# The weight sums of a seven-product output projection, made by transfers that add to their target

## The chip, the cores and the metric

The kernel runs on one core of a Trainium2 chip. A core has a matrix engine (TensorE, PE in the profile, with a weight-load side PEld), a vector engine (VectorE, DVE), a scalar engine (ScalarE, ACT), a general engine (GpSimd, POOL) and SyncE (SP), which here only issues transfers. They run their own instruction lists and meet at semaphores. The metric is the device time of one execution in microseconds; a comparison goes by the median of several executions.

## The reference

One layer: an input projection, two token mixers side by side, a gated merge, one output projection and a layer norm over residual plus projection. Everything is float32. The part that the change touches is the second and third line from the end:

```
ua = jnp.einsum('blc,cd->bld', (oa.astype(x.dtype) * jax.nn.silu(za)), w_up_a)
ub = jnp.einsum('blc,cd->bld', ob * jax.nn.silu(zb), w_up_b)
merged = jax.nn.sigmoid(ga) * ua + jax.nn.sigmoid(gb) * ub
y = jnp.einsum('bld,de->ble', merged, w_out)
return layer_norm(ALPHA * x + y, ln_g, ln_b)
```

There are 512 tokens and 1024 channels, so `merged` is 512 x 1024 and `w_out` 1024 x 1024.

## The kernel before

A float32 product is made of three matmuls of rounded parts. Each operand is split into a high part (rounded to the matmul's format, by ACT) and a low part (the operand less its high part, by DVE or GpSimd); the three matmuls are high x high, high x low and low x high. So every weight, and every sum of weights, costs a transfer, a rounding on ACT and a subtraction on GpSimd or DVE before TensorE can use it.

The work is cut into units of 256 output columns (`UNITS`); unit `u` is quartered, and a quarter number `q` = 4u to 4u + 3 is the clock by which each engine's program is written: at each `q` every engine does what its `side(q)` and the tables (`OUT_HI_AT`, `OUT_HI_THEN`, `OUT_LO_AT`) say. The last units, `up0` to `up3` (q = 108 to 123), are the two up-projections. Their results are merged on DVE (`merge(m)`, m = 0 to 7, 128 channels each) into `mix`, rounded on ACT (`round_merged`), and given a low part on DVE (L1739). `sum_rows(j)` makes four sums of quarters of `mix` into `s_raw`, `round_sums(j)` rounds them (L1208), and `sum_rows_lo(j)` makes their low part (L1762).

The output projection is a 2 x 2 block product done with seven block products instead of eight (the Strassen-Winograd scheme): token halves and even or odd channels on one side, four blocks `b11`, `b12`, `b21`, `b22` of `w_out` on the other. The products run in the order `b11`, `b21`, `t1`, `t2`, `b22`, `t3`, `t4` (`OUT_WEIGHTS`). Each is 24 matmuls: two token tiles (`i`) of four pieces (`j`) of three matmuls, L965 to L968. The four `t` are sums of weight blocks:

- t1 = b12 - b11, t2 = b22 - t1, t3 = b22 - b12, t4 = b21 - t2, each one made by DVE in `sum_out` (L1783) from blocks of 128 x 2048 floats, 1 MB.

`out_raw(name)` says where a raw block or sum lies: `z_a`, `z_b`, or one of the two halves of `w_raw`, the ring through which the weight units come. SP loads the blocks with `load_out` (L586): `b11` and `b12` before `up0`, `b12` again into `z_a` once b11's low parts are done, `b21` once the low parts of `up2` are done and `b22` after those of `up3`. ACT rounds block n in two halves, `split_out_hi(n, half)` (L1224). GpSimd makes the low part in four pieces, `split_out_lo(n, piece)` (L2072). Both have an order of their own, `HI_ORDER` and `LO_ORDER`, in which b22 comes before t2. ACT is in order: in its program behind the last quarter stand `round_merged(7)`, `keep_first` (L1229, a copy of product b11 to `first_sum`, which product b21 waits for before it adds to the same bank), `round_sums(3)`, the roundings of t2, t3 and t4, and then `move_u` (L1234), which copies the partial sum `u` to the bank in which product t3 goes on; t3 waits for it (`u_moved`).

In the tail each token block t gets its row statistics on DVE (L1793, L1796), 1 / sigma on ACT, and is scaled by halves: on DVE (`normalise_half`, L1840 and L1843), or, for the halves in `ON_POOL`, by one operation on ACT and two on GpSimd.

Of the kernel before, what the change touches and what calls it, by code (L numbers as in the profile page):

```python
# [115 lines left out]
def hybrid_kernel(nc, x_t, x_tok, w_units, w_kiwi, b_cols, b_ia, b_vb, lb_cols, g_cols, rel_bias,  # L116
                  ln_g, ln_b, one_hot, ident, causal, tree_masks, out):
    with ExitStack() as ctx:
# [179 lines left out]
        out_in = {n: sem(f"out_in_{n}") for n in OUT_BLOCKS}  # L298
        out_sum, out_hi, out_lo, out_lo_dve = (sem(n) for n in ("out_sum", "out_hi", "out_lo", "out_lo_dve"))
# [175 lines left out]
        def out_raw(name):  # L475

            u2, u3 = UNITS.index("up2"), UNITS.index("up3")
            ring = {"b21": u2, "t4": u2, "b22": u3}
            if name in ring:
                return w_raw[:, ring[name] % 2, :].rearrange("p (j n) -> p j n", j=PAIRS)  # L480
            return z_a[:] if name in ("b11", "t3") else z_b[:]

        def wait_out_raw(eng, name):

            if name in OUT_BLOCKS:
                eng.wait_ge(out_in[name], 16)
            else:
                eng.wait_ge(out_sum, ("t1", "t2", "t3", "t4").index(name) + 1)

        LO_ORDER = (0, 1, 2, 4, 3, 5, 6)  # L490
# [11 lines left out]
        HI_ORDER = (0, 1, 2, 4, 3, 5, 6)  # L502
# [60 lines left out]
        def _(sp):  # L563
# [21 lines left out]
            def load_out(name, dst):  # L585
                sp.dma_start(dst, w_units[NMAIN - 1 + OUT_BLOCKS.index(name)]  # L586
                             .rearrange("p (j n) -> p j n", j=PAIRS)).then_inc(out_in[name], 16)

            for u in range(2, NMAIN):
                if UNITS[u] == "up0":  # L590
                    sp.wait_ge(o_lo_done, 4)
                    load_out("b11", z_a[:])
                    load_out("b12", z_b[:])
# [380 lines left out]
        def _(act):  # L974
# [342 lines left out]
            for q in range(4 * NMAIN):  # L1317
# [10 lines left out]
                for v in range(3, NMAIN):  # L1328
                    if q - hi_quarter(v) in (0, 1):
                        split_hi(v, q - hi_quarter(v))  # L1330
# [26 lines left out]
                if m is not None:  # L1357
                    round_merged(m)
                    if m % 2:
                        round_sums(m // 2)  # L1360
# [22 lines left out]
        def _(dve):  # L1383
# [358 lines left out]
            def sum_rows(j):  # L1742

                if j:
# [4 lines left out]
                nc.vector.tensor_tensor(s_raw[:, 0, :], even[:, HALF:], odd[:, HALF:], ALU.add).then_inc(s_raw_done, 1)  # L1749
# [7 lines left out]
                                        ALU.subtract).then_inc(s_raw_done, 1)  # L1757
# [6 lines left out]

            def sum_out(name):

                dst = out_raw(name)
                if name == "t1":
                    wait_out_raw(dve, "b11")
                    wait_out_raw(dve, "b12")  # L1770
                    a, b = z_b[:], z_a[:]
                elif name == "t2":
                    wait_out_raw(dve, "b22")
                    wait_out_lo(dve, 2, 4)
                    a, b = out_raw("b22"), z_b[:]
                elif name == "t3":
                    dve.wait_ge(out_in["b12"], 32)
                    a, b = out_raw("b22"), z_a[:]
                else:
                    wait_out_lo(dve, 1, 4)  # L1780
                    dve.wait_ge(out_sum, 2)
                    a, b = out_raw("b21"), out_raw("t2")
                nc.vector.tensor_tensor(dst, a, b, ALU.subtract).then_inc(out_sum, 1)  # L1783
# [34 lines left out]
            def rows_12(i):  # L1818
# [6 lines left out]
                nc.vector.tensor_tensor(c12_bank[i][:], c12_bank[i][:], u_sum[:, i, :], ALU.add).then_inc(pre_12, 1)  # L1825

            def rows_22(i):

                t = 2 + i
                wait_y_full(dve, "t3", i)  # L1830
                link(nc.vector.tensor_tensor(m6_bank[i][:], c21_bank[i][:], y_sb[:, t, 512:], ALU.add))
                with_residual(c21_bank[i][:], t, 0, c21_bank[i][:]).then_inc(pre_21, 1)
                row_stats(t, 1)
# [18 lines left out]
            def side(q):  # L1852
# [70 lines left out]
                if q == T1_AT:  # L1923
                    sum_out("t1")
# [61 lines left out]
        def _(pool):  # L1986
# [79 lines left out]

            def split_out_lo(n, piece):
# [4 lines left out]
                nc.gpsimd.tensor_tensor(lo, out_raw(name)[:, piece, :], hi.bitcast(F32), ALU.subtract).then_inc(out_lo, 1)  # L2072

# [8 lines left out]
            for q in range(4 * NMAIN):  # L2082
                side(q)
                for n, piece in OUT_LO_AT.get(q, ()):
                    split_out_lo(n, piece)
            for n in LO_ORDER[3:]:
                for piece in range(4):
                    split_out_lo(n, piece)
            pool.wait_ge(ln_in, 32)
# [73 lines left out]
```

## Time and profile before

| | us |
|---|---|
| median of three executions | 460.0 (459.72 to 460.41) |
| the profiled execution | 459.87 |
| its span, first to last instruction | 457.8 |
| what lies around the span | 2.1 |

The profile is one execution. The page gives each engine's busy time; the views in order of time give each instruction's start and duration in us from the start of the span, and, in square brackets, how long its engine stood idle before it and what ended that. The duration of an instruction on DVE or GpSimd includes what it stands for access to its data. Matmuls overlap: one is shown with 0.39 us but the next begins 0.23 us later. For a transfer the view shows the issue; the time to landing stands in the table of issues.

### The profile page before, as it was taken

How to read it: one execution, taken by the hardware profiler on the slowest of the kernel's cores; microseconds unless marked ns; L12 is line 12 of the kernel's file. 1: busy time of each engine (PE TensorE's matmuls, PEld its weight loads, DVE VectorE, ACT ScalarE, POOL GpSimd, SP SyncE). 2: the span in 40 equal slices, each digit the busy share in tenths (PEclk: the TensorE clock that was granted, in tenths of full speed). 3: DMA queues.
4: the chain of work that ended last, by engine and by line, in shares of the span. 5: the costliest groups of instructions: out<-in, count | busy, mean ns of one | idle time of the engine just before them, and what ended most of it. 6: DMA issues, size and time to landing. Idle time of an engine off the chain costs nothing.

```text
span 457.8 us, 7703 instructions
## 1 busy us (share of the span) xinstructions
PE 445.2 (97%) x2946; PEld 362.8 (79%) x2946; DVE 319.7 (70%) x585; ACT 236.7 (52%) x398; POOL 186.3 (41%) x175
## 2 busy tenths in 40 slices
PE   9999999999999999999999999999999999999793
PEld 7778888888888788888888887887888888877582
DVE  4546589999999853346989994870642058899977
ACT  5735455253345746285777475735775343624421
POOL 0444432582259813581004000000066494655962
PEclk9999999999999999999999999999999999999997
DMA  8808122256023620205020222041066254231013
GB/s 255 297 23 295 69 79 93 92 155 214 0 93 98 179 94 1 93 1 169 16 94 1 95 93 93 1 129 59 1 226 227 99 181 186 93 130 55 0 46 137
DMA packets 16867, 48.77 MB, mean 107 GB/s; under 512 B 2456, under 2 KB 4288, under 8 KB 16192
## 3 DMA queue, kind: packets, MB, share of 16 engines
q1 hardware_dynamic: 16592, 48.10, 31.5%
q8 instruction: 23, 0.38, 0.3%
q10 hardware_dynamic: 240, 0.20, 0.2%
q14 instruction: 12, 0.10, 0.1%
HBM read 44.09 MB, written 2.11 MB: 101 GB/s over the span
## 4 chain that ended last, share of the span: by engine, by line
PE 85%; DVE 9%; POOL 2%; issue 2%; ACT 2%; DVEq 0%; POOLq 0%
PE bank L635 21%; PE bank L636 21%; PE bank L637 21%; PE bank L798 2%; PE bank L783 2%; POOL w_lo L2072 2%; PE bank L881 2%; PE bank L834 2%; DVE s_lo L1762 1%; PE bank L774 1%; PE bank L773 1%; PE bank L965 1%; PE bank L968 1%; PE bank L967 1%; PE bank L925 1%
## 5 line engine op out<-in xcount | busy, mean ns | idle before, releaser
L1998 POOL TENSOR_TENSOR w_lo<-w_raw,w_hi 128x512 fp32r<-128x512 f32 x84 | 112.3, 1363 | 157.2 <-ACT w_hi L976 157.1
L635 PE MATMUL bank<-x_hi,w_hi 128*128 128x512 f32 x336 | 133.0, 396 | 0.0
L636 PE MATMUL bank<-x_lo,w_hi 128*128 128x512 f32 x336 | 131.2, 390 | 0.0
L637 PE MATMUL bank<-x_hi,w_lo 128*128 128x512 f32 x336 | 130.9, 390 | 0.0
L635 PEld LDWEIGHTS bank<-x_hi,w_hi 128*128 128x128 f32 x336 | 63.1, 188 | 13.9 <-issue 0.8
L637 PEld LDWEIGHTS bank<-x_hi,w_lo 128*128 128x128 f32 x336 | 63.1, 188 | 13.6
L636 PEld LDWEIGHTS bank<-x_lo,w_hi 128*128 128x128 f32 x336 | 63.1, 188 | 12.2
L976 ACT ACTIVATE w_hi<-w_raw 128x1024 fp32r<-128x1024 f32 (+2 forms) x63 | 62.5, 1012 | 8.0 <-PE bank L637 5.7
L1063 ACT ACTIVATE prob<-prob,nmax 128x128 f32<-128x128 f32 (+3 forms) x32 | 17.7, 555 | 41.6 <-DVE nmax L1517 41.5
L1493 DVE MAX8 best<-score 128x8 f32<-128x256 f32 (+2 forms) x48 | 26.8, 559 | 1.1
L1505 DVE COPY prob_t<-bank 128x128 f32<-128x128 f32 (+3 forms) x32 | 14.3, 486 | 19.0 <-PE bank L783 18.9
L1494 DVE MATCH_REPLACE8 score<-best,score 128x256 f32<-128x256 f32 (+2 forms) x48 | 26.1, 543 | 0.0
L635 PE MATMUL bank<-w_hi,x_hi 128*128 128x512 f32 x64 | 25.3, 395 | 0.0
L637 PE MATMUL bank<-w_hi,x_lo 128*128 128x512 f32 x64 | 25.0, 390 | 0.0
L636 PE MATMUL bank<-w_lo,x_hi 128*128 128x512 f32 x64 | 24.9, 390 | 0.0
L635 PE MATMUL bank<-o_hi,w_hi 128*128 128x512 f32 x64 | 24.9, 389 | 0.0
L636 PE MATMUL bank<-o_lo,w_hi 128*128 128x512 f32 x64 | 24.9, 389 | 0.0
L637 PE MATMUL bank<-o_hi,w_lo 128*128 128x512 f32 x64 | 24.9, 389 | 0.0
L1053 ACT ACTIVATE relus<-bank 128x256 f32<-128x256 f32 (+2 forms) x24 | 10.5, 489 | 21.2 <-PE bank L763 21.2
L2016 POOL TENSOR_TENSOR logit<-t,pen 128x256 f32<-128x256 f32 x24 | 17.4, 737 | 9.1 <-DVE nmax L1517 9.1
L1483 DVE SCALAR_TENSOR_TENSOR score<-relus,w_idx,score 128x256 f32<-128x256 f32 (+2 forms) x21 | 15.6, 743 | 7.8 <-ACT relus L1053 6.1
L1697 DVE TENSOR_TENSOR w_lo<-w_raw,w_hi 128x512 fp32r<-128x512 f32 x32 | 20.6, 684 | 0.0
(267 smaller groups left out, 824.2 us busy)
## 6 DMA issues: line engine op xcount, KB each, us to landing
w_raw<-in_w_units SPq DMA_DIRECT2D x58, 512.0 KB, 4.7
z_a<-in_w_units SPq DMA_DIRECT2D x2, 1024.0 KB, 5.2
w_raw<-in_w_units SPq DMA_DIRECT2D x2, 1024.0 KB, 4.8
y_sb<-in_x_tok SPq DMA_DIRECT2D x4, 512.0 KB, 4.7
out<-y_sb SPq DMA_DIRECT2D x8, 256.0 KB, 2.0
x_raw_hi<-in_x_t SPq DMA_DIRECT2D x4, 256.0 KB, 5.2
x_raw_lo<-in_x_t SPq DMA_DIRECT2D x4, 256.0 KB, 6.3
t_turned<-t_row SPq DMA_DIRECT2D x1, 1024.0 KB, 9.7
```

The costliest lines, as they stand in the source:

```text
L635: nc.tensor.matmul(dst, a_hi, b_hi, start=first, stop=False)
L636: nc.tensor.matmul(dst, a_hi, b_lo, start=False, stop=False)
L637: return nc.tensor.matmul(dst, a_lo, b_hi, start=False, stop=last)
L976: nc.scalar.activation(split_target(u, kiwi_hi, x_hi, w_hi)[:, k, :], raw(u)[:, k, :], ACT.Copy).then_inc(done, 1)
L1063: nc.scalar.activation(prob[:, i % 4, 0:n], prob[:, i % 4, 0:n], ACT.Exp, bias=nmax[:, i % 4:i % 4 + 1], scale=-1.0, accum_out=prob_sum[:, ...
L1483: ins = nc.vector.scalar_tensor_tensor(out=score[b][:], in0=relus[:, i % 2, 0:n], scalar=w, in1=score[b][:], op0=ALU.mult, op1=ALU.add)
L1493: link(nc.vector.max(best8[:], score[b][:]))
L1494: link(nc.vector.match_replace(score[b][:], best8[:], score[b][:], TAKEN))
L1505: nc.vector.tensor_copy(prob_t[:, i % 4, 0:n], turn_bank[i % 2][:, 0:n]).then_inc(turn_out[i % 2], 1)
L1697: nc.vector.tensor_tensor(split_target(u, kiwi_lo, x_lo, w_lo)[:, k, :], raw(u)[:, k, :], split_target(u, kiwi_hi, x_hi, w_hi)[:, k, :].bi ...
L1998: nc.gpsimd.tensor_tensor(split_target(u, kiwi_lo, x_lo, w_lo)[:, k, :], raw(u)[:, k, :], split_target(u, kiwi_hi, x_hi, w_hi)[:, k, :].bi ...
L2016: nc.gpsimd.tensor_tensor(logit[:, i % 2, n - band:n], t5[:, h, 2 * P - band:], pen[b][:, n - band:] if b else causal_sb[:], ALU.add).then ...
```

## The change

The signs of the scheme are turned so that all sums of weights are additions: t1 = b12 + b11, t2 = b22 + b11 + b12, t3 = b12 + b22, t4 = b11 + b12 + b22 + b21. On the other side some sums of `mix` and three sums of results turn from add to subtract or back, on the same shapes. `sum_out` and its four calls on DVE are gone. In their place GpSimd issues transfers that add a block from memory to what already lies in the target (`add_block`, `accum_op=ALU.add`): one for t1, two for t2, three for t4, one for t3. Each waits for the load of its target and for the add before it to the same target. SP loads the first term: `b22` as t2 into `z_a`, `b11` as t4 into the ring half in which b21 lay, `b12` as t3 into `z_b`, the last two ahead of the loads of `y_sb`. The orders `HI_ORDER` and `LO_ORDER` become plain 0 to 6, so t2 is split ahead of b22. Both halves of the rounding of `up3` go to q = 116, the rounding of b21 goes from q = 118 to q = 116 and ahead of `round_sums`, its low parts from 119 to 118. Of token block 1 both halves are now scaled by GpSimd.

```
-OUT_HI_THEN = {118: ((1, 0), (1, 1))}
-OUT_LO_AT = {110: ((0, 0), (0, 1), (0, 2), (0, 3)), 119: ((1, 0), (1, 1), (1, 2), (1, 3)), 121: ((2, 2), (2, 3))}
-T1_AT, T1_LO_AT = 106, 121
-ON_POOL = ((), (1,), (1,), ())
+OUT_HI_THEN = {116: ((1, 0), (1, 1))}
+OUT_LO_AT = {110: ((0, 0), (0, 1), (0, 2), (0, 3)), 118: ((1, 0), (1, 1), (1, 2), (1, 3)), 121: ((2, 2), (2, 3))}
+ADD_AT = {101: (("t1", "b11"),), 114: (("t2", "b11"),), 117: (("t2", "b12"),), 121: (("t4", "b12"),)}
+T1_LO_AT = 121
+ON_POOL = ((), (0, 1), (1,), ())
...
+        TERMS = {"t1": 2, "t2": 3, "t3": 2, "t4": 4}
...
             wait_out_lo(sp, 0, 4)
-            sp.wait_ge(out_sum, 1)
-            load_out("b12", z_a[:])
+            load_out("t2", "b22")
             wait_lo(sp, UNITS.index("up2"), 4)
-            load_out("b21", out_raw("b21"))
+            load_out("b21", "b21")
             wait_lo(sp, UNITS.index("up3"), 4)
-            load_out("b22", out_raw("b22"))
+            load_out("b22", "b22")
+            wait_out_lo(sp, 1, 4)
+            load_out("t4", "b11")
+            wait_out_lo(sp, 2, 4)
+            load_out("t3", "b12")
...
-            split_out_hi(4, 0)
-            split_out_hi(4, 1)
+            split_out_hi(3, 0)
+            split_out_hi(3, 1)
             round_merged(KT - 1)
             keep_first(0)
             keep_first(1)
             round_sums(PAIRS - 1)
-            for n in (3, 5, 6):
+            for n in (4, 5, 6):
                 for half in range(2):
                     split_out_hi(n, half)
...
             sum_rows(PAIRS - 1)
-            sum_out("t2")
             sum_rows_lo(PAIRS - 1)
-            sum_out("t3")
             dve.wait_ge(ln_in, 32)
             rows_11(0)
-            sum_out("t4")
             rows_11(1)
...
+            def add_block(name, block):
+
+                pool.wait_ge(out_in[name], 16)
+                if added[name]:
+                    pool.wait_ge(out_add[name], 16 * added[name])
+                added[name] += 1
+                nc.gpsimd.dma_start(out_raw(name), out_block(block), accum_op=ALU.add).then_inc(out_add[name], 16)
...
             for n in LO_ORDER[3:]:
                 for piece in range(4):
                     split_out_lo(n, piece)
+                if n == 3:
+                    add_block("t4", "b22")
+                    add_block("t3", "b22")
+                elif n == 4:
+                    add_block("t4", "b21")
```

The first place is ACT's list from the rounding of `up3` (`w_hi<-w_raw`) to that of `mix` 5. A name in brackets is what the instruction waits for. Before:

```order
L976 ACTIVATE w_hi<-w_raw 128x1024 [waits part_done,w_in0_0]
L1203 ACTIVATE odd_hi<-mix 128x512 [waits mix_done]
L1208 ACTIVATE s_hi_hi<-s_raw 128x1024 [waits s_raw_done]
L976 ACTIVATE w_hi<-w_raw 128x1024 [waits w_in0_1]
L1203 ACTIVATE even_hi<-mix 128x256 [waits mix_done]
L1224 ACTIVATE x_hi<-w_raw 128x1024 [waits part_done,out_in_b21]
L1224 ACTIVATE x_hi<-w_raw 128x1024
L1224 ACTIVATE w_hi<-z_b 128x1024 [waits part_done,out_sum]
L1224 ACTIVATE w_hi<-z_b 128x1024
L1203 ACTIVATE odd_hi<-mix 128x512 [waits mix_done]
```

And after the change:

```order
L983 ACTIVATE w_hi<-w_raw 128x1024 [waits part_done,w_in0_0]
L983 ACTIVATE w_hi<-w_raw 128x1024 [waits w_in0_1]
L1210 ACTIVATE odd_hi<-mix 128x512 [waits mix_done]
L1231 ACTIVATE x_hi<-w_raw 128x1024 [waits part_done,out_in_b21]
L1231 ACTIVATE x_hi<-w_raw 128x1024
L1215 ACTIVATE s_hi_hi<-s_raw 128x1024 [waits s_raw_done]
L1210 ACTIVATE even_hi<-mix 128x256 [waits mix_done]
L1231 ACTIVATE w_hi<-z_b 128x1024 [waits part_done,out_add_t1,out_in_t1]
L1231 ACTIVATE w_hi<-z_b 128x1024
L1210 ACTIVATE odd_hi<-mix 128x512 [waits mix_done]
```

The second half of `up3` and both halves of b21 (`x_hi<-w_raw`) stand now ahead of the rounding of the s sums (`s_hi_hi<-s_raw`), with b21's load (`out_in_b21`) as a wait in front of it.

The second place is GpSimd's list from the low parts of b21 (`x_lo<-w_raw`) to those of t4, the last ones. Before:

```order
L2072 TENSOR_TENSOR x_lo<-w_raw,x_hi 128x512 [waits out_hi] x4
L2072 TENSOR_TENSOR w_lo<-z_b,w_hi 128x512 [waits out_hi] x2
L2072 TENSOR_TENSOR w_late<-w_raw,w_late 128x512 [waits out_hi] x4
L2072 TENSOR_TENSOR w_lo<-z_b,w_hi 128x512 [waits out_hi] x4
L2072 TENSOR_TENSOR x_lo<-z_a,x_hi 128x512 [waits out_hi] x4
L2072 TENSOR_TENSOR x_lo<-w_raw,x_hi 128x512 [waits out_hi] x4
```

And after the change, from the last low part of `up3` on:

```order
L1984 TENSOR_TENSOR w_lo<-w_raw,w_hi 128x512 [waits hi_done]
L2060 TENSOR_TENSOR x_lo<-w_raw,x_hi 128x512 [waits out_hi] x4
L2060 TENSOR_TENSOR w_lo<-z_b,w_hi 128x512 [waits out_hi] x2
L2068 DMA w_raw<-in_w_units 128x2048 [waits out_in_t4]
L2060 TENSOR_TENSOR w_lo<-z_a,w_hi 128x512 [waits out_hi] x4
L2068 DMA w_raw<-in_w_units 128x2048 [waits out_add_t4,out_in_t4]
L2068 DMA z_b<-in_w_units 128x2048 [waits out_in_t3]
L2060 TENSOR_TENSOR w_late<-w_raw,w_late 128x512 [waits out_hi] x4
L2068 DMA w_raw<-in_w_units 128x2048 [waits out_add_t4,out_in_t4]
L2060 TENSOR_TENSOR x_lo<-z_b,x_hi 128x512 [waits out_hi] x4
L2060 TENSOR_TENSOR x_lo<-w_raw,x_hi 128x512 [waits out_hi] x4
```

Four of the seven adding transfers (`DMA ... <-in_w_units`) stand between the low parts, each behind the waits in its brackets, and the low parts of t2 (`w_lo<-z_a`) have moved ahead of those of b22 (`w_late`).

## Rows read from the trace of the kernel before

**Rows 1.** Busy time by engine, from the page (busy us, share, instructions).

```profile
PE 445.2 (97%) x2946; PEld 362.8 (79%) x2946; DVE 319.7 (70%) x585; ACT 236.7 (52%) x398; POOL 186.3 (41%) x175
```

**Rows 2.** TensorE in order of time (start us, us, line, operation; idle before).

```profile
406.77 0.39 PE L965 MATMUL bank<-x_hi,even_hi 128*128 128x512 f32 x1
...
408.58 0.39 PE L968 MATMUL bank<-x_hi,even_lo 128*128 128x512 f32 x1
409.96 0.50 PE L965 MATMUL bank<-x_hi,even_hi 128*128 128x512 f32 x1 [0.98 <-DVE even_lo L1739]
...
413.30 0.39 PE L968 MATMUL bank<-x_hi,even_lo 128*128 128x512 f32 x1
414.23 0.50 PE L965 MATMUL bank<-x_hi,odd_hi 128*128 128x512 f32 x1 [0.54 <-ACT first_sum L1229]
...
426.39 0.40 PE L968 MATMUL bank<-w_hi,s_lo 128*128 128x512 f32 x1
429.07 0.50 PE L965 MATMUL bank<-w_hi,s_hi_lo 128*128 128x512 f32 x1 [2.28 <-POOL w_lo L2072]
...
429.64 0.39 PE L968 MATMUL bank<-w_hi,s_lo 128*128 128x512 f32 x1
430.32 0.50 PE L965 MATMUL bank<-w_hi,s_hi_lo 128*128 128x512 f32 x1 [0.29 <-POOL w_lo L2072]
...
449.98 0.39 PE L968 MATMUL bank<-x_hi,odd_lo 128*128 128x512 f32 x1
```

**Rows 3.** VectorE (DVE) in order of time, 401 to 425 us.

```profile
401.04 1.50 DVE L1749 TENSOR_TENSOR s_raw<-mix 128x256 f32<-128x256 f32 x1
...
406.92 0.69 DVE L1732 TENSOR_TENSOR bank<-bank,gate_a_lo 128x512 f32<-128x512 f32 x1
...
417.71 2.28 DVE L1783 TENSOR_TENSOR z_b<-w_raw,z_b 128x2048 f32<-128x2048 f32 x1
...
421.04 2.29 DVE L1783 TENSOR_TENSOR z_a<-w_raw,z_a 128x2048 f32<-128x2048 f32 x1
...
424.70 3.18 DVE L1783 TENSOR_TENSOR w_raw<-w_raw,z_b 128x2048 f32<-128x2048 f32 x1
```

**Rows 4.** ScalarE (ACT) in order of time, 391 to 433 us.

```profile
391.00 1.06 ACT L1208 ACTIVATE s_hi_hi<-s_raw 128x1024 fp32r<-128x1024 f32 x1 [2.33 <-DVE s_raw L1756]
...
427.92 2.01 ACT L1224 ACTIVATE x_hi<-w_raw 128x1024 fp32r<-128x1024 f32 x2 [2.55 <-DVE w_raw L1783]
432.62 0.60 ACT L1234 ACTIVATE bank<-u_sum 128x512 f32<-128x512 f32 x1 [2.70 <-DVE u_sum L1822]
```

**Rows 5.** GpSimd (POOL) in order of time, 421 to 435 us.

```profile
421.17 9.10 POOL L2072 TENSOR_TENSOR w_lo<-z_b,w_hi 128x512 fp32r<-128x512 f32 x4 [4.79 <-ACT w_hi L1224]
430.22 5.03 POOL L2072 TENSOR_TENSOR x_lo<-z_a,x_hi 128x512 fp32r<-128x512 f32 x4
```

**Rows 6.** SP, the queue that issues transfers, in order of time.

```profile
384.95 11.23 SPq L586 DMA_DIRECT2D w_raw<-in_w_units  x2
406.96 1.75 SPq L623 DMA_DIRECT2D y_sb<-in_x_tok  x4
```

**Rows 7.** Issues (KB each, us to landing) and two windows (DMA share, GB/s last).

```profile
z_a<-in_w_units SPq DMA_DIRECT2D x2, 1024.0 KB, 5.2
...
z_b<-in_w_units SPq DMA_DIRECT2D x1, 1024.0 KB, 6.8
...
338.00:348.00 10.00, 10.00 (x46) 8.29 (x45) 2.70 (x2) 6.01 (x7) 7.06 (x5) 1.00 0.84 315
384.00:396.00 12.00, 12.00 (x55) 9.94 (x54) 10.57 (x14) 6.00 (x7) 6.37 (x6) 1.00 0.25 89
```

**Rows 8.** VectorE in order of time, the last 11 us of the span.

```profile
447.11 0.76 DVE L1840 SCALAR_TENSOR_TENSOR bank<-bank,aggr,ln_gb 128x512 f32<-128x512 f32 x1
447.90 0.75 DVE L1843 SCALAR_TENSOR_TENSOR y_sb<-bank,rstd,ln_gb 128x512 f32<-128x512 f32 x1
...
451.00 0.69 DVE L1793 BATCH_NORM_STATS2 stats<-bank 128x6 f32<-128x512 f32 x1
```

More of the change, by code:

```diff
@@ L480, in out_raw, with out_block @@
                 return w_raw[:, ring[name] % 2, :].rearrange("p (j n) -> p j n", j=PAIRS)
-            return z_a[:] if name in ("b11", "t3") else z_b[:]
+            return z_a[:] if name in ("b11", "t2") else z_b[:]
+        def out_block(name):
+            return w_units[NMAIN - 1 + OUT_BLOCKS.index(name)].rearrange("p (j n) -> p j n", j=PAIRS)
+        TERMS = {"t1": 2, "t2": 3, "t3": 2, "t4": 4}
         def wait_out_raw(eng, name):
[L485 to L490, printed above, removed]
+            eng.wait_ge(out_in[name], 16)
+            if name in TERMS:
+                eng.wait_ge(out_add[name], 16 * (TERMS[name] - 1))
+        LO_ORDER = (0, 1, 2, 3, 4, 5, 6)
         def wait_out_lo(eng, n, pieces):
@@ L591, in _ @@
                     sp.wait_ge(o_lo_done, 4)
-                    load_out("b11", z_a[:])
-                    load_out("b12", z_b[:])
+                    load_out("b11", "b11")
+                    load_out("t1", "b12")
                 if u >= 3:
@@ L1328, in _ @@
                 for v in range(3, NMAIN):
-                    if q - hi_quarter(v) in (0, 1):
+                    if v == NMAIN - 1 and q == hi_quarter(v):
+                        split_hi(v, 0)
+                        split_hi(v, 1)
+                    elif v < NMAIN - 1 and q - hi_quarter(v) in (0, 1):
                         split_hi(v, q - hi_quarter(v))
@@ L1358, in _ @@
                     round_merged(m)
-                    if m % 2:
-                        round_sums(m // 2)
                 for n, half in OUT_HI_THEN.get(q, ()):
                     split_out_hi(n, half)
-            split_out_hi(4, 0)
-            split_out_hi(4, 1)
+                if m is not None and m % 2:
+                    round_sums(m // 2)
+            split_out_hi(3, 0)
+            split_out_hi(3, 1)
             round_merged(KT - 1)
@@ L1748, in sum_rows @@
                 n = 4 * j
-                nc.vector.tensor_tensor(s_raw[:, 0, :], even[:, HALF:], odd[:, HALF:], ALU.add).then_inc(s_raw_done, 1)
+                nc.vector.tensor_tensor(s_raw[:, 0, :], even[:, HALF:], odd[:, HALF:],
+                                        ALU.subtract).then_inc(s_raw_done, 1)
                 nc.vector.tensor_tensor(s_raw[:, 2, :], even[:, 0:HALF], even[:, HALF:],
@@ L1756, in sum_rows @@
                 nc.vector.tensor_tensor(s_raw[:, 3, :], odd[:, 0:HALF], s_raw[:, 1, :],
-                                        ALU.subtract).then_inc(s_raw_done, 1)
+                                        ALU.add).then_inc(s_raw_done, 1)
             def sum_rows_lo(j):
@@ L1763, in sum_rows_lo @@
                                         ALU.subtract).then_inc(s_lo_done, 1)
[L1765 to L1783, printed above, removed]
             def first_sum_lo():
@@ L1824, in rows_12 @@
                 dve.wait_ge(early_12, i + 1)
-                nc.vector.tensor_tensor(c12_bank[i][:], c12_bank[i][:], u_sum[:, i, :], ALU.add).then_inc(pre_12, 1)
+                nc.vector.tensor_tensor(c12_bank[i][:], c12_bank[i][:], u_sum[:, i, :], ALU.subtract).then_inc(pre_12, 1)
             def rows_22(i):
@@ L1830, in rows_22 @@
                 wait_y_full(dve, "t3", i)
-                link(nc.vector.tensor_tensor(m6_bank[i][:], c21_bank[i][:], y_sb[:, t, 512:], ALU.add))
+                link(nc.vector.tensor_tensor(m6_bank[i][:], y_sb[:, t, 512:], c21_bank[i][:], ALU.subtract))
                 with_residual(c21_bank[i][:], t, 0, c21_bank[i][:]).then_inc(pre_21, 1)
@@ L2065, in side @@
                         far_factors(p)
+            added = {name: 0 for name in TERMS}
             def split_out_lo(n, piece):
@@ L2085, in _ @@
                     split_out_lo(n, piece)
+                for name, block in ADD_AT.get(q, ()):
+                    add_block(name, block)
             for n in LO_ORDER[3:]:
```

14 lines of the change are left out of this document (6 added, 8 removed).

## The prediction, made before the changed kernel had run

> **What bounds the kernel now.** I read the page's busy times first. TensorE is busy 445.2 us of a span of 457.8 us [rows 1], so a change that leaves the matmuls alone can win only where TensorE stands idle, or after its last matmul. Next I listed TensorE's instructions of the last 60 us in order of time [rows 2]. The output projection begins at 406.77. Nine matmuls later (408.58) the pace is (408.58 - 406.77) / 8 = 0.226 us each, so one of the seven products, 24 matmuls, takes 5.44 us when nothing stops it. Against that pace there are four gaps: 408.58 + 0.23 to 409.96 is 1.15 us (the low half of `mix` 6, from DVE), 413.30 + 0.23 to 414.23 is 0.70 us (`first_sum`), 426.39 + 0.23 to 429.07 is 2.45 us, and 429.64 + 0.23 to 430.32 is 0.45 us. The last two are product t2 waiting for the low parts of its weight sum. Together they are 4.75 us. The last matmul ends at 449.98 + 0.39 = 450.37, and the 7.4 us to the end of the span belong to the layer norm and the last store.
>
> Why t2 is late is in the other engines' rows. DVE makes the sum t2 from 417.71, t3 from 421.04, t4 from 424.70, 2.3 to 3.2 us each [rows 3]. ACT rounds t2 after its sum, and GpSimd's four low parts take 9.10 us from 421.17, where the next four take 5.03 us, 1.26 us each [rows 5]: the big DVE sums and GpSimd's operations get in each other's way.
>
> **What the change removes.** First, the three late sums on DVE, 2.28 + 2.29 + 3.18 = 7.75 us [rows 3], and an earlier one, t1. With them goes the late t2: its raw sum comes from transfers issued around 385 and 394, ACT rounds it right behind the last projection (after 406.8), and GpSimd makes its low parts before those of b22. From 409 four pieces, even at the slowed 9.10 us, end by 418, while TensorE reaches t2 at 406.77 + 3 x 5.44 = 423.1 or later. Both t2 gaps go: **-2.90 us**. What is late next is discussed under t3. Sign changes (subtract for add, on equal tiles) cost nothing: the same DVE operation on the same shape.
>
> Second, both halves of token block 1's last scaling now go to GpSimd. DVE no longer does 0.76 + 0.75 us there at 447.11 and 447.90 [rows 8]. The statistics of the last block start at 451.00, though TensorE ended at 450.37; with 1.5 us less ahead of them they start 0.6 us sooner: **-0.6 us**. ACT's second scaling and GpSimd's two further operations fit before 451.
>
> **What it adds.** Seven adding transfers of 1 MB from GpSimd's queue, and two more plain 1 MB loads. No row shows a transfer from GpSimd or an adding one. The nearest row is a plain load of the same bytes: 5.2 us from issue to landing alone, 6.8 us with another just ahead [rows 7]. The window 338 to 348 moved 315 GB/s at a DMA share of 0.84, that is 375 GB/s at full share; 1.05 MB then need 2.8 us of moving, and 5.2 - 2.8 = 2.4 us are fixed. An adding transfer has a source to read like the load, and its target to read besides. So its moving time is between 2.8 us (the target's read hidden) and 5.6 us (the two reads one after the other), and an adder slower than the stream would go above it. I take 4.0 us, between the ends, because one of the two reads stays on the chip and never meets the weight loads at their source; both ends are kept. The issue on GpSimd I take at 1 us, between an SP issue (0.33 us) and a GpSimd tile operation (1.26 us).
>
> Now the places. *The first add* (t1) is issued near 348 and needed at 396: hidden at any of these sizes. *The second and third* (t2 += b11, t2 += b12): the first goes out at about 385, together with SP's load of b21 (384.95 [rows 6]). Sharing the engines, that load lands near 385 + 2.4 + 2 x 2.8 = 393 instead of 390. This matters because ACT's rounding of b21 has been moved ahead of the rounding of the s sums, which ran at 391.00 [rows 4]. ACT now stands at b21 from 389 to 393, rounds 2 us, and the s sums come at 395 instead of 391. Queued behind are DVE's low part of the s sums and the merges of `mix` 4 and 5; both move back by some 2.7 us, and then the four small s sums (1.50 us where GpSimd is busy, as at 401.04 [rows 3]) follow. The merge of `mix` 6, at 406.92 in the trace, comes 0.8 to 1.5 us later, and TensorE's gap for it grows from 1.15 to some 2.0 us: **+0.9 us**. The 0.70 us gap stays.
>
> *t4 and t3* are the tight ones. In the new order the load of t4 goes out when b21's low parts are done (403) and lands at 408; t4 += b12 is issued at about 409 beside the load of t3 and the four loads of `y_sb` (406.96 in the trace [rows 6]), so it moves at half speed and lands at 409 + 8.0 + 2.4, near 419. Then t4 += b22 and t3 += b22 go out, and move one after the other: t4 near 426.5, t3 near 430.5. t4 += b21 is issued when b22's low parts are done, near 427, and lands behind t3 at 434.7. ACT rounds t4 (2.01 us, as at 427.92) and only then moves `u` into the bank (0.60 us, as at 432.62 [rows 4]), and product t3 waits for that move. So t3 can start at 434.7 + 2.0 + 0.6 + 0.1 = 437.4. TensorE comes to it at 406.77 + 5 x 5.44 + 2.0 + 0.7 = 436.7 with the gaps above and two or three tenths of slow restarts. The chain ends within half a microsecond of the need: at 4.0 us of moving time it costs **0 to +0.5 us**, at 2.8 us nothing. I put it at 0.
>
> **Sum**, on the profiled execution (459.87 us, span 457.8): -2.90 - 0.6 + 0.9 + 0 = -2.6, so 457.3 us. The profiled execution lies 0.13 us under the median of 460.0, so the forecast is **457.4 us**.
>
> **Rivals.** (A) *The adding transfers are nearly as cheap as loads* (2.8 to 3.3 us). Then b21 and the t4 chain both have room, the +0.9 shrinks to about 0, and even the 1.15 us gap goes, since the sums left DVE and ACT is on time; 460.0 - 2.9 - 0.6 - 1.15 = 455.4 us. For it: engines were far from full (DMA share 0.25 from 384 to 396 [rows 7]). Against: two reads. (B), *on the other side: the t4 chain takes the place of t2*. The decisive point is a moving time of about 4.4 us. Above it, each further microsecond counts four to five times, since four adds stand in a row before the rounding of t4 (one of them at half speed) and the move of `u` stands behind it. At 5.6 us the last add lands near 443 and t3 starts near 445.7, while TensorE, its `mix` 6 gap grown by 1.5 us, comes to it at 437.3: 8.4 us of standing, and 460.0 - 2.9 - 0.6 + 1.5 + 8.4 = **466 us**; at 4.8 us the same count gives about 461.5. For it: nothing hides the second read if the engines are full, and y loads, t3 load and adds together ask for 3 x 2.8 + 4 x 5.6 = 31 us of moving in the 28 us from 409 to 437. Against: the share of the target's read that overlaps the source's. The Trainium skill, "Collectives: The Full Stack", in "The bandwidth ceiling: the fold count and why AG ≠ RS ≠ AR", says a reducing transfer reads two sources on one ring and runs at half a copy's rate; by that rule the time would be that of rival B, and no row here shows it. (C) *The third place:* the adds go out later than issued, because GpSimd's own descriptor work meets DVE; it would look like B, and is in its chance. (D) The change does not relieve t2 or the wins and losses cancel: 459.1 to 460.9.
>
> **How the numbers follow.** The forecast (moving time 3.5 to 4.3 us, 456 to 459 us) gets 0.33, rival A 0.17, D 0.10, B 0.40: some 0.24 of it up to 467, the rest above. The likeliest single case is faster, though its lead is small, so the range must hold both signs: from 455.0 (just under A's time) to 467.0 (B with the two reads one after the other), which leaves out an adder slower than that. The forecast's own range is 456 to 459. Bounds of 0.2% (0.9 us) are about what a measurement of this kernel tells from no change: faster 0.50, same 0.10, slower 0.40.
>
> **What would show it.** Right: no gap of TensorE before t2's matmuls; t2's low parts on GpSimd done by 418; the adding transfers landing 7 to 8 us after issue; the end of the last matmul 2 us sooner and the tail 0.6 us shorter. Wrong: a gap before the first matmul of t3 with ACT's `u` move as releaser and t4's last add landing after 436 (B); a gap over 2.5 us in b11 (the b21 rounding costs more than said); GpSimd standing more than 1 us per issue.

## The result, and the profile of the changed kernel

The changed kernel takes 467.61 us (median of four executions, 465.59 to 468.75) where the kernel before took 460.21 us beside it. The ratio is 1.015, with a 95% interval of 1.0127 to 1.0172. The forecast was 457.4 us with a range up to 467.0: wrong in its sign and just outside its range. The profiled execution took 468.75 us with a span of 466.9 us, 9.1 us more than the 457.8 before. It is the slowest of the four (the medians differ by 7.4 us): its mean granted clock is 0.981, that of the others 0.986 to 0.991, so the books below are those of this one execution. Two executions of the experiments further down (746.7 and 904.07 us) fell in a second, much slower state and are left out of all medians and ratios.

TensorE in order of time, to be read beside [rows 2] (start us, us, line, operation; idle before and what ended it):

```profile
406.79 0.39 PE L972 MATMUL bank<-x_hi,even_hi 128*128 128x512 f32 x1
...
408.60 0.39 PE L975 MATMUL bank<-x_hi,even_lo 128*128 128x512 f32 x1
413.14 0.80 PE L972 MATMUL bank<-x_hi,even_hi 128*128 128x512 f32 x1 [4.15 <-DVE even_lo L1749]
413.73 0.63 PE L974 MATMUL bank<-x_lo,even_hi 128*128 128x512 f32 x1
...
418.58 0.39 PE L974 MATMUL bank<-x_lo,even_hi 128*128 128x512 f32 x1
...
440.57 0.39 PE L975 MATMUL bank<-w_late,s_lo 128*128 128x512 f32 x1
446.43 0.80 PE L972 MATMUL bank<-x_hi,s_hi_hi 128*128 128x512 f32 x1 [5.48 <-ACT bank L1241]
...
452.48 0.39 PE L975 MATMUL bank<-x_hi,s_lo 128*128 128x512 f32 x1
...
459.99 0.39 PE L975 MATMUL bank<-x_hi,odd_lo 128*128 128x512 f32 x1
```

The output projection starts where it did (406.79, before 406.77). The two gaps before t2 and the one of `first_sum` are gone, 2.90 and 0.70 us. Two others are in their place: 4.31 us before the tenth matmul of the output projection (1.15 before) and 5.63 us before product t3 (none before). Behind each, most matmuls follow each other at 0.43 us instead of 0.227: the 13 from 413.14 to 418.58 take 5.44 us where 2.95 is the pace, the 14 from 446.43 to 452.48 take 6.05 us where 3.18 is. The clock column names it (windows; the granted clock is the first of the last three columns, then DMA share and GB/s):

```profile
412.00:418.00 6.00, 4.86 (x11) 3.81 (x12) 4.72 (x7) 3.43 (x5) 4.84 (x5) 0.50 0.98 317
...
440.00:450.00 10.00, 4.52 (x13) 3.27 (x12) 2.50 (x5) 3.44 (x6) 8.03 (x7) 0.78 0.24 61
```

A granted 0.50 is the level of 1.2 GHz, and TensorE had stood for 4.3 us ahead of it. (The second window holds the gap and the end of the half clock, hence its 0.78.) The books, then: -2.90 - 0.70 + 3.16 (the gap of `mix` 6) + 2.49 (half clock behind it) + 5.63 (the gap of t3) + 2.87 (half clock) - 0.9 (the tail: 466.9 - 460.38 = 6.5 us, before 7.4) = +9.65 against a measured +9.1. The half microsecond left over is in the kernel before: from its first to its last matmul start of the output projection are 449.98 - 406.77 = 43.21 us, and 167 steps of 0.227 us with the gaps of 4.75 us make only 42.66. Most of the rest is in the slower first steps behind its four gaps (0.34 us each instead of 0.227, as behind 409.96).

### The profile page after: what moved, and what is told of

The parts are those of the page before. It is cut to its first block, busy times and chain, and to the rows that moved or that the text cites. A ratio compares the mean times of both kernels' runs of the same rounds, so it can differ in the third digit from the quotient of the medians.

```text
span 466.9 us, 7708 instructions
## 1 busy us (share of the span) xinstructions
PE 449.7 (96%) x2946; PEld 366.8 (79%) x2946; DVE 311.6 (67%) x579; ACT 237.6 (51%) x399; POOL 187.4 (40%) x184
## 4 chain that ended last, share of the span: by engine, by line
PE 83%; DMA 10%; POOL 2%; DVE 2%; issue 2%; ACT 1%; POOLq 0%; DVEq 0%
PE bank L642 21%; PE bank L643 20%; PE bank L644 20%; DMA w_raw<-in_w_units 7%; DMA z_a<-in_w_units 3%; PE bank L790 2%; PE bank L805 2%; PE bank L888 2%; PE bank L841 2%; PE bank L781 1%; PE bank L780 1%; PE bank L972 1%; POOL x_lo L2060 1%; PE bank L974 1%; PE bank L932 1%
## 5 line engine op out<-in xcount | busy, mean ns | idle before, releaser
L1984 POOL TENSOR_TENSOR w_lo<-w_raw,w_hi 128x512 fp32r<-128x512 f32 x84 | 111.1, 1349 | 153.3 <-ACT w_hi L983 153.2
L1742 DVE TENSOR_TENSOR bank<-bank,gate_a_hi 128x512 f32<-128x512 f32 x4 | 2.8, 694 | 32.2 <-PE bank L644 32.2
## 6 DMA issues: line engine op xcount, KB each, us to landing
w_raw<-in_w_units POOLq DMA_DIRECT2D x3, 1024.0 KB, 11.3
y_sb<-in_x_tok SPq DMA_DIRECT2D x4, 512.0 KB, 12.4
```

Source lines behind the costliest of these rows:

```text
L1984: nc.gpsimd.tensor_tensor(split_target(u, kiwi_lo, x_lo, w_lo)[:, k, :], raw(u)[:, k, :], split_target(u, kiwi_hi, x_hi, w_hi)[:, k, :].bi ...
```

## The two gaps, read in the other engines' rows

**The gap of 4.31 us.** DVE and GpSimd in order of time, to be read beside [rows 3] and [rows 5]:

```profile
396.11 0.70 DVE L1742 TENSOR_TENSOR bank<-bank,gate_a_lo 128x512 f32<-128x512 f32 x1
...
398.89 8.69 DVE L1749 TENSOR_TENSOR odd_lo<-mix,odd_hi 128x512 fp32r<-128x512 f32 x1 [0.70 <-ACT odd_hi L1210]
...
410.10 0.69 DVE L1742 TENSOR_TENSOR bank<-bank,gate_a_lo 128x512 f32<-128x512 f32 x1
```

```profile
397.34 0.88 POOL L2068 DMA_DIRECT2D z_a<-in_w_units  x1 [6.65 <-DMA z_a<-in_w_units]
397.95 1.59 POOL L1984 TENSOR_TENSOR w_lo<-w_raw,w_hi 128x512 fp32r<-128x512 f32 x1
399.21 5.32 POOL L2060 TENSOR_TENSOR x_lo<-w_raw,x_hi 128x512 fp32r<-128x512 f32 x4
404.20 2.82 POOL L2060 TENSOR_TENSOR w_lo<-z_b,w_hi 128x512 fp32r<-128x512 f32 x2
```

The merge of `mix` 5 began at 396.11, earlier than before (396.83). But its subtraction for the low part, which took 1.51 us in the kernel before (at 399.60), stood for 8.69 us. The GpSimd rows tell when it was let go: GpSimd stood until t2's first addition had landed (397.34), issued the second, and then ran seven tile operations without a break from 397.95 to 407.02. DVE's subtraction, there from 398.89, was over at 407.58. The merge of `mix` 6 came at 410.10 instead of 406.92.

**The gap of 5.63 us.** The chain of work that ended last (start us, us):

```profile
384.89 11.91 DMA z_a<-in_w_units
397.34 0.88 POOL z_a L2068
398.23 1.32 POOL w_lo L1984
399.55 4.99 POOL x_lo L2060 x4
404.55 6.79 DMA w_raw<-in_w_units
411.63 11.88 DMA w_raw<-in_w_units
424.06 7.94 DMA w_raw<-in_w_units
432.53 6.41 DMA w_raw<-in_w_units
438.94 4.95 issue
443.89 2.01 ACT x_hi L1231 x2
446.43 0.80 PE bank L972
```

Transfer behind transfer: the load of t4's first term, three additions to it, the rounding of t4 on ACT, and behind it on ACT the move of `u` for which t3 waits. The issues and two windows stand against [rows 7]; the first window is of the changed kernel, in a stretch in which nearly only additions moved (1.26 of 1.37 MB), the second of the kernel before while it only loaded:

```profile
w_raw<-in_w_units POOLq DMA_DIRECT2D x3, 1024.0 KB, 11.3
...
y_sb<-in_x_tok SPq DMA_DIRECT2D x4, 512.0 KB, 12.4
425.00:432.00 7.00, 7.00 (x33) 5.79 (x32) 3.90 (x6) 0.00 (x0) 5.88 (x5) 1.00 1.01 196
```

```profile
340.00:346.00 6.00, 6.00 (x28) 4.98 (x27) 0.64 (x1) 4.31 (x5) 3.06 (x4) 1.00 0.98 391
```

With its DMA engines full, the core loads 391 GB/s and adds 196: half. 1.05 MB at 196 GB/s are 5.35 us of moving. Stretches with additions alone gave 192 GB/s (433 to 440 us here) and 213 (425 to 432 us with t2's second addition one place later, below), so the term lies between 4.9 and 5.5 us. The last addition to t4 was issued at 432.53; two of the three took 11.88 and 7.94 us, so the median of 11.3 is the third, and it landed at 443.8. The 4.95 us of "issue" in the chain are that wait: ACT had ended t3's rounding at 438.94 and the view lost the releaser. The Trainium skill, "Collectives: The Full Stack", in "The bandwidth ceiling: the fold count and why AG ≠ RS ≠ AR", gives the reducing step of a ring of cores, which reads two sources, about half the rate of its copying step; the adding transfers of this one core agree with that ratio (196 against 391).

## Experiments

Each kernel was timed in 3 or 5 rounds beside the kernel before, which had medians of 460.9 to 461.5 us there; so the ratios can be compared. It had 460.2 us beside the changed kernel, so a difference of two absolute times from here and there is good to about a microsecond. Each trace is that of one execution.

**Copies in place of additions.** The mode of adding is left out, so the t sums are not made; places, sizes and waits stay.

```
-nc.gpsimd.dma_start(out_raw(name), out_block(block), accum_op=ALU.add)
+nc.gpsimd.dma_start(out_raw(name), out_block(block))
```

> The changed kernel with the seven transfers from GpSimd as plain copies: same places, waits and bytes, no adding (so t1 to t4 hold one block each instead of a sum: the additions are left out). Theory (the second read of an adding transfer is what costs): a copy lands 5 to 7 us after its issue instead of 10.3 to 11.3, t4's last term lands near 433, both large gaps of TensorE go, 455 to 457 us. Rival (transfers issued by GpSimd are slow whatever they do, or GpSimd's waits are the loss): landing stays near 10 us, the time within 2 us of the changed kernel's 467.6.

Measured: 460.51 us, ratio 0.999 [0.9976, 1.0005]. The copies landed in 5.0 to 8.4 us, the three into t4's place in 5.0 us each (the additions there took 11.9, 7.9 and 11.3), and the gap before t3 is gone with its half clock: the price of adding is that chain. But the time did not come to 455, for the other gap stayed, a little earlier (DVE, GpSimd and TensorE in order of time):

```profile
394.77 7.95 DVE L1749 TENSOR_TENSOR even_lo<-mix,even_hi 128x256 fp32r<-128x256 f32 x1 [0.48 <-ACT even_hi L1210]
```

```profile
393.07 0.57 POOL L2068 DMA_DIRECT2D z_a<-in_w_units  x1 [2.19 <-DMA z_a<-in_w_units]
393.66 1.30 POOL L1984 TENSOR_TENSOR w_lo<-w_raw,w_hi 128x512 fp32r<-128x512 f32 x1
394.92 5.04 POOL L2060 TENSOR_TENSOR x_lo<-w_raw,x_hi 128x512 fp32r<-128x512 f32 x4
```

```profile
405.90 0.79 PE L642 MATMUL bank<-o_hi,w_hi 128*128 128x512 f32 x1 [4.20 <-DVE mix L1746]
```

So a long stand of DVE's subtraction comes without adding too.

**The move of `u` ahead of t4's rounding.** On ACT, in the changed kernel:

```
-for n in (4, 5, 6): split_out_hi(n, 0), split_out_hi(n, 1)
-move_u(0), move_u(1)
+for n in (4, 5): split_out_hi(n, 0), split_out_hi(n, 1)
+move_u(0), move_u(1)
+split_out_hi(6, 0), split_out_hi(6, 1)
```

> The changed kernel with one edit on ScalarE: the two moves of u that product t3 waits for stand ahead of the rounding of t4 instead of behind it. Theory (the t4 chain of adds reaches TensorE through ScalarE's order): in the changed kernel u was ready at 436 and t3's low parts began at 438, so t3 starts when TensorE arrives at 440.6, t4's first low part is there at 446.3 against an arrival at 446.0. The gap of 5.6 us and the 2.7 us of half clock behind it go, 8.4 us together: 459.2 us. Rival (the adds into t3 and t4 are late in themselves, whatever ScalarE's order): the gap moves to t3's or t4's low parts, and the time stays within 1 us of the changed kernel, 466 to 468.

Measured: 464.91 us (median of three), ratio 1.0094 [1.006, 1.0127], where 459.2 was expected. The gap of t3 went (0.43 us left), and 3.07 us came before t4, with 13 matmuls at half clock behind them:

```profile
450.33 0.79 PE L972 MATMUL bank<-x_hi,odd_hi 128*128 128x512 f32 x1 [2.92 <-DVE bank L1794]
```

```profile
445.91 0.75 DVE L1836 SCALAR_TENSOR_TENSOR y_sb<-bank,rstd,ln_gb 128x512 f32<-128x512 f32 x1 [5.73 <-ACT rstd L1248]
```

DVE waited 5.73 us for the first root, which also stands behind t4's rounding on ACT. The late sum of t4 holds whatever ACT has behind it, and taking one thing out of its way brought up the next.

**The tail alone.** The kernel before with `ON_POOL = ((), (0, 1), (1,), ())`.

> The kernel before with ON_POOL alone changed, so GpSimd scales both halves of token block 1. Theory: the last block's statistics start 0.6 us sooner and nothing else moves: 459.6 us against 460.2. Rival (the tail is set by the last store or by GpSimd's own last operations): no difference, 460.2 +- 0.2.

Measured: 460.08 us (median of eleven), ratio 0.9985 [0.9968, 1.0001], so 0.7 us and just not told apart from nothing.

**Additions for t1 and t2 alone**, with DVE's sums of t3 and t4 and the tables of the kernel before.

> A version between the two: t1 and t2 are made by adding transfers and t2 is split ahead of b22, as in the change; t3 and t4 are made by VectorE as t3 = b22 + b12 and t4 = b21 + t2, with no adds after q = 117; ScalarE's and GpSimd's tables for up3 and b21 as before. Theory (adds with slack are free, only the t4 chain and what stands behind GpSimd's waits cost): t2's gaps of 2.9 us go, the tail gives 0.6, the mix 6 gap of 1.15 us stays: 456.5 to 457.5. Rival (the adds into t2 alone already hold GpSimd and delay mix 6 by more than t2 gives back): a gap over 3 us in b11 as in the changed kernel, and 460 us or more.

Measured: 462.15 us, ratio 1.0027 [1.001, 1.0044]. The gaps of t2 are gone. The slowed place beside DVE's big sums is now that of b22's low parts (9.24 us for four), but these end at 432.15 and hold nothing. What holds b22, for 2.01 us, is DVE's row work (the addition of `u_sum` to a bank), which stands behind its sums of t3 and t4 (3.38 and 3.18 us). And the long subtraction is here too (8.46 us, gap 4.08).

**t2's second addition one place later.** In the changed kernel:

```
-117: (("t2", "b12"),)
+118: (("t2", "b12"),)
```

> The changed kernel with one number moved: t2's second addition stands in GpSimd's program at quarter 118, behind the low parts of b21, instead of at 117, so that the last low part of up3 and those of b21 are not held back behind the landing of t2's first addition. Theory 1 (VectorE's subtraction for mix 5 stood 8.7 us because GpSimd ran a backlog that had piled up behind its wait): the subtraction takes at most 3 us, mix 6 is ready 3 to 4 us earlier, the gap of 4.3 us before b21 and its 11 matmuls at half clock go, and the time is 461 to 463 us (467.6 less 4 to 6.5); the t3 gap of 5.6 us stays. Theory 2 (the subtraction stands whenever GpSimd has six tile operations in a row behind an issue of a transfer): it still takes over 6 us and the time stays within 1.5 us of 467.6.

Measured: 459.99 us, ratio 0.9989 [0.9974, 1.0004]: 7.6 us for one number. The subtraction took 0.79 us and the gap before b11's tenth matmul is gone; 1.43 us stand in the last up-projection instead. And more came than was expected, since GpSimd's low parts of b21 were no longer held: they ended at 397.7 instead of 404.6, the first addition to t4 went out at 403.92 instead of 411.63, and t3's gap fell from 5.63 to 3.17 us, its matmuls at half clock from 13 to 7. GpSimd, then a row of DVE:

```profile
386.53 5.70 POOL L1984 TENSOR_TENSOR w_lo<-w_raw,w_hi 128x512 fp32r<-128x512 f32 x4 [0.67 <-ACT w_hi L983]
392.19 5.56 POOL L2060 TENSOR_TENSOR x_lo<-w_raw,x_hi 128x512 fp32r<-128x512 f32 x4
397.69 0.87 POOL L2068 DMA_DIRECT2D z_a<-in_w_units  x1
```

```profile
402.11 0.79 DVE L1749 TENSOR_TENSOR odd_lo<-mix,odd_hi 128x512 fp32r<-128x512 f32 x1 [0.70 <-ACT odd_hi L1210]
```

**The loads of `y_sb` behind the first addition to t4.** SP gets `sp.wait_ge(out_add["t4"], 16)` ahead of them.

> The changed kernel with the four loads of y_sb made to wait for the first addition to t4. Theory 1 (an adding transfer of 1 MB needs 10 us in itself, reading two sources): t4's first addition still lands 10 us or more after its issue, the t3 gap stays over 4.5 us, and the time is within 1.5 us of 467.6. Theory 2 (it took 11.9 us because the loads of y_sb and of t3 shared the DMA engines with it): it lands in at most 8.5 us, the chain of t4 ends 3 us or more earlier, and the time is 462 to 465 us.

Measured: 470.01 us, ratio 1.0205 [1.0179, 1.023]. The first addition still took 10.63 us against 11.88, so sharing with these loads was a minor part of it; it still went beside the load of t3's first term. The loads of `y_sb` moved in among the next additions, the row work on DVE came late, and now product b22 waits 6.26 us for it. Two rows of the chain:

```profile
410.74 10.63 DMA w_raw<-in_w_units
422.76 16.25 DMA y_sb<-in_x_tok
```

**What makes the subtraction stand.** Four variants of the kernel before, in which nothing is added by a transfer, were made to tell. First, a wait alone that gives GpSimd the same backlog: behind q = 117, `pool.wait_ge(a_done, 6)`.

> The kernel before with nothing but one wait added: GpSimd holds up3's last low part and what stands behind it until VectorE has made its first product for mix 5 (about 397.5 us), as the wait for t2's first addition held it in the changed kernel; no transfer is issued by GpSimd and nothing is added. Theory 1 (the backlog behind a wait is the cause): VectorE's subtraction for mix 5 stands 6 us or more until GpSimd has run all six or seven tile operations, a gap of about 4 us appears before b21 and with it some matmuls at half clock, and the time is 464 to 467 us. Theory 2 (the issue of a transfer on GpSimd just ahead, or memory traffic of the additions, is the cause): the subtraction takes at most 3 us as in the kernel before, and the time is within 1 us of 460.5.

Measured: 461.73 us, ratio 1.0018 [1.0003, 1.0034]. No operation stood for long: DVE and GpSimd took turns.

```profile
398.70 1.10 DVE L1739 TENSOR_TENSOR odd_lo<-mix,odd_hi 128x512 fp32r<-128x512 f32 x1 [0.70 <-ACT odd_hi L1203]
399.71 1.51 DVE L1749 TENSOR_TENSOR s_raw<-mix 128x256 f32<-128x256 f32 x1
```

Theory 1 (the backlog) fell. Next, the same wait, with two plain loads of 512 KB (`ln_gb`) issued behind it by GpSimd instead of by SP.

> The kernel before with the hold of the earlier run (GpSimd waits for VectorE's first product for mix 5) and with the two small loads of the LayerNorm's gain and shift issued by GpSimd right behind it instead of by SP; nothing is added by a transfer. Theory 3 (what makes VectorE's subtraction stand is an issue of a transfer by GpSimd directly ahead of tile operations that run without a wait; the hold alone did not do it): it stands 6 us or more, the gap before b21 is 3.5 us or more with matmuls at half clock, and the time is 464 to 466 us. Theory 4 (it takes the large transfers of the additions or copies moving at that time): the subtraction takes at most 2 us, the gap is about 2 to 3 us (the two issues delay GpSimd by 1 to 2 us), and the time is 461 to 463 us.

Measured: 463.36 us, ratio 1.0054 [1.0036, 1.0071], gap 4.43 us, 12 matmuls at half clock. DVE, then GpSimd:

```profile
398.64 8.80 DVE L1737 TENSOR_TENSOR odd_lo<-mix,odd_hi 128x512 fp32r<-128x512 f32 x1 [0.70 <-ACT odd_hi L1201]
```

```profile
397.60 0.53 POOL L2088 DMA_DIRECT2D ln_gb<-in_ln_b  x1
398.14 1.31 POOL L1996 TENSOR_TENSOR w_lo<-w_raw,w_hi 128x512 fp32r<-128x512 f32 x1
399.40 5.01 POOL L2070 TENSOR_TENSOR x_lo<-w_raw,x_hi 128x512 fp32r<-128x512 f32 x4
```

The issues without the wait:

> The kernel before with those two small loads issued by GpSimd between up3's third and last low parts, without the hold. Theory 3: GpSimd issues them at about 394.4 to 396, then runs its seven tile operations without a wait, and a VectorE operation that arrives within that run stands until its end, 5 us or more; 463 to 466 us. Theory 4: all VectorE operations there take at most 2.5 us, as in the kernel before, and the time is 460 to 461.5 us.

Measured: 466.43 us, ratio 1.0109 [1.0085, 1.0133]. Another DVE operation (`s_lo`) came while GpSimd was still issuing (394.66 to 395.90), was not done when the run began, and stood 10.80 us; the gap was 6.12 us.

```profile
394.93 10.80 DVE L1760 TENSOR_TENSOR s_lo<-s_raw,s_hi_hi 128x1024 fp32r<-128x1024 f32 x1
```

Last, the issues first and the wait between them and the run:

> The kernel before with the two small loads issued by GpSimd between up3's third and last low parts, and the hold (the wait for VectorE's first product for mix 5) behind them, so that GpSimd waits between the issue and the run of tile operations. Theory 3 in its strict form (the run has to follow the issue without a wait): no VectorE operation stands over 2.5 us, the gap before b21 is about 2 us as with the hold alone, and the time is 461 to 462 us. Rival (one issue by GpSimd is enough for what comes later): a VectorE operation stands 6 us or more, and the time is 463 to 466 us.

Measured: 462.3 us, ratio 1.002 [1.0003, 1.0037]. The same `s_lo`, again beside the issues, took 1.21 us, and the subtraction 1.10 us, as with the wait alone. DVE, then GpSimd:

```profile
394.74 1.21 DVE L1760 TENSOR_TENSOR s_lo<-s_raw,s_hi_hi 128x1024 fp32r<-128x1024 f32 x1
...
399.02 1.10 DVE L1737 TENSOR_TENSOR odd_lo<-mix,odd_hi 128x512 fp32r<-128x512 f32 x1 [0.70 <-ACT odd_hi L1201]
```

```profile
395.19 0.53 POOL L2087 DMA_DIRECT2D ln_gb<-in_ln_b  x1
397.02 1.29 POOL L1996 TENSOR_TENSOR w_lo<-w_raw,w_hi 128x512 fp32r<-128x512 f32 x1 [1.30 <-DVE bank L1730]
398.29 5.84 POOL L2070 TENSOR_TENSOR x_lo<-w_raw,x_hi 128x512 fp32r<-128x512 f32 x4
```

In these kernels it takes an issue by GpSimd with tile operations directly behind it. Adding, the size of the transfer (512 KB or 1 MB) and a wait ahead of the issue are not needed. Whether the wait itself or the time it takes parts the two was not tried; in the run with t2's second addition one place later, 0.67 us of waiting behind the issue of 384.97 were enough, and DVE's operations beside the eight tile operations that followed took 1.4 to 1.5 us each. Nor does every DVE operation stand: in the changed kernel GpSimd issued two additions (424.06, 424.64) and ran four operations directly behind them, while DVE's operations there, with at most one input in SBUF and one in a bank, took their usual 0.70 us. The four operations on `x_lo` show the same from GpSimd's side: 5.01 us where they follow the issue, 5.84 us where DVE gets its turns.

**Additions for t1 and t2 alone, the second one place later.**

> Additions by transfer for t1 and t2 alone; t3 and t4 are summed on VectorE as in the kernel before; t2's second addition at quarter 118, behind the low parts of b21. If theory 1 on the backlog holds: no long subtraction, the gap before b21 at most 1.5 us, the two gaps before t2 (2.9 us) gone, one gap of about 2 us before b22 left, and the time is 456.5 to 459 us. If the subtraction stands anyway (theory 2): 461.5 to 463 us, as the run with t2's addition at quarter 117.

Measured: 461.14 us, ratio 1.0003 [0.9989, 1.0018]. It agrees with the four variants: here GpSimd waited 1.21 us for the first addition, issued the second at 397.14 and ran straight on with `x_lo` at 397.75, and the subtraction at 399.70 stood 6.38 us (gap 2.74). One place later helps only where the issue comes behind the run.

**Both small changes together**: quarter 118, and the move of `u` first.

> Both small changes together on the changed kernel: t2's second addition behind the low parts of b21 (quarter 118), and ScalarE moves u into its banks ahead of rounding t4. Theory (the two sites are independent, and t4's sum, which landed at 433.4 us with the first change alone, is now early enough): the gap of 3.2 us before t3 and its 7 matmuls at half clock go, no gap over 1 us comes before t4, and the time is 455 to 456 us against 460.0 with the first change alone. Rival (t4 takes t3's place as it did in the run with the second change alone): a gap of 1.5 to 3 us before t4, and 458 to 460 us.

Measured: 457.66 us, ratio 0.9936 [0.9916, 0.9955]. The gap of t3 is gone; 2.05 us stand before t4, with no matmul at half clock behind them. The time lies between the theory and its rival, since a gap before t4 was left as the rival said, by the road that moving `u` alone had shown. The expectation also read one row wrongly: with the first change alone t4's last addition was issued at 426.95 and took 9.2 us, so it landed at 436.2 and not at 433.4 (where ACT's rounding of t3 had ended), and here at 435.9. So ACT's rounding of t4, and the root behind it, were still late:

```profile
442.94 0.50 PE L972 MATMUL bank<-x_hi,odd_hi 128*128 128x512 f32 x1 [1.89 <-DVE bank L1794]
```

**And the first root ahead of t4's rounding** (`root(0)` behind `move_u(1)` on ACT):

> The combined version (t2's second addition at quarter 118, u moved ahead of t4's rounding) with one step more: ScalarE also takes the first row block's root ahead of t4's rounding, in the 1.9 us in which it stands idle there, so that VectorE does not wait for that root until 438.4 us and comes to C21's rows earlier. Theory: the gap of 2.05 us before t4, which VectorE's late row operation ends, shrinks to at most 0.5 us, and the time is 455.5 to 456.5 us (0.989 of before). Rival (something else stands right behind, such as the low parts of t4 on GpSimd, which end at 442.3 us): the gap stays over 1.2 us and the time is over 457 us.

Measured: 455.74 us (455.39 to 456.4), ratio 0.9887 [0.9868, 0.9906]. No matmul at half clock and no gap over half a microsecond is left in the output projection; 1.42 us stand in the last up-projection, where the kernel before has none. It is the fastest version: 1.1% under the kernel before.

## Why the prediction was wrong, step by step

Three terms of the sum failed: the moving time of an addition (4.0 us, measured 5.35), with it the chain of t4 (0 us, measured 5.63 us of standing and 2.87 at half clock), and `mix` 6 (+0.9 us, measured +3.16 and 2.49 at half clock), whose cause was not in the prediction at all.

- **t2's gaps, -2.90 us:** right. The low parts of t2 ran from 413.67, ended at 419.55 (forecast: by 418), and no matmul of t2 waited.
- **The tail, -0.6 us:** -0.9 in the trace. By itself it gave 0.7 us, not told apart from nothing, and a tail 0.5 us shorter in that trace; the size fits, and the times do not show it.
- **The issue, 1 us:** right, 0.88 us (0.57 us for a copy).
- **The moving time, taken as 4.0 us between 2.8 and 5.6:** mis-sized. It is 5.35 us (4.9 to 5.5). The reason given ("one of the two reads stays on the chip") was an argument without a row, and the upper end was nearly the truth. The decisive point was put at 4.4 us, so by the prediction's own working the t4 chain had to take t2's place. Rival B at 5.6 us said: last addition lands near 443, t3 starts near 445.7, 466 us. Measured: 443.8, 446.43, 467.6.
- **t4's chain, 0 us:** wrong by 5.63 us of standing, and by 2.87 us at half clock. It also began late, the first addition at 411.63 and not at 409, as b21's low parts on GpSimd had been held up. That the clock can fall behind a gap was in no term of the sum; the gaps of before, up to 2.45 us, had no such matmuls behind them.
- **`mix` 6, +0.9 us (1.15 to 2.0):** wrong in size and in mechanism. ACT's rounding of b21 began at 390.96 and ended at 392.97, not 395, and the merge of `mix` 5 was no later than before. The gap grew to 4.31 us, with 2.49 us at half clock behind it, because DVE stood behind GpSimd's run. The prediction wrote of GpSimd's waits only what they cost the transfers. It put t2's second addition at 394 (issued at 397.34, since the first took 11.9 us), and named neither what is queued on GpSimd behind that wait nor that DVE could stand for a whole run.
- **`first_sum`, stays at 0.70 us:** wrong, gone.

Rival B's time came out, but its agreement is in part chance: B had 8.4 us of standing before t3, 1.5 us more at `mix` 6 and nothing at half clock, where the trace has 5.63, 3.16 and 5.36 us. Since the gap of `mix` 6 held TensorE itself back, the chain of t4 had less to show. Rival A (455.4 us, cheap additions) gave a number near that of the last experiment, by another road. The forecast's own number, 457.4, is also near that of the kernel with t2's second addition later and `u` moved first (457.66), and that is luck too: the additions are no cheaper there (213 GB/s, 4.9 us), but t4's chain began 8.2 us earlier (403.41) and less stood behind t4 on ACT.

## What to carry to other kernels

An adding transfer moved at half the rate of a load here: count two loads of the DMA engines' time for each, and where several go one after the other into one target, start the first as early as the target is free. On GpSimd put the issue of a transfer behind its run of tile operations, or ahead of a wait, and not directly ahead of the run while VectorE has operations with both inputs in SBUF. And when an engine that works in order has to wait for a late result, look for what stands behind it that does not need it: moving three such things ahead (the low parts of b21, the move of `u`, a root) took the time from 1.015 to 0.989 of the kernel before. A gap of TensorE can cost more than its length, by what runs at half clock behind it.

## What the runs showed of the hardware that was not expected

- **A VectorE operation with both inputs in SBUF stood through a whole run of GpSimd's operations.** It stood 6.38 to 10.80 us in all eight profiles in which such a run directly followed an issue by GpSimd and such an operation met it (8.69 in the changed kernel; 7.95, 8.41, 8.46, 8.50, 6.38, 8.80 and 10.80 in the variants), until the six or seven operations of some 1.3 us had ended. With a wait between (1.10 us) or without an issue (1.10 us) the engines took turns. The Trainium skill, "SBUF — State Buffer", in "Who interferes with whom", says that a VectorE instruction with two SBUF inputs contends with a GpSimd instruction that reads SBUF, and that the second to come is blocked until the first has finished. The turns of about 1.5 us agree with that. The long stands go beyond one instruction, and why an issue ahead of the run changes it is open.
- **Adding against loading:** 196 (192 to 213) against 391 GB/s with the DMA engines full; the issue on GpSimd 0.88 against 0.57 us.
- **TensorE's clock behind a gap:** after 4.31 and 5.63 us of standing the granted clock was 0.50 for 11 and 13 matmuls, 2.49 and 2.87 us lost beyond the gap. Behind 4.03 to 6.26 us in the variants it was 7 to 13. Behind shorter gaps it went either way: 13 matmuls at half clock behind 3.07 us and 7 behind 3.17; none behind 2.45 us in the kernel before, none behind 2.05 with both small changes, but 8 behind 2.01 us with additions for t1 and t2 alone and 8 behind 2.07 us in the run with the issues first, each time after some at full clock. What decides it was not tried.
- **Small loads pay too:** the `y_sb` loads of 512 KB took 12.4 us instead of 4.7 among the additions.
